# Experts fed by 512-column units of gate, then of up, and their activations turned one unit later

## The chip, the cores and the metric

The kernel runs on one core of a Trainium2 chip. The metric is the device time of one execution in microseconds (us), lower is better. Engines: TensorE (PE, with its weight loads PEld), VectorE (DVE), ScalarE (ACT), GpSimd (POOL) and SyncE (SP, here the queue that issues nearly all loads).

## What is computed

Two transformer blocks over 256 tokens of width 1024, in float32. The second layer of the first block ends in a mixture of experts, and that is the part that changes:

```python
def swiglu(h, wg, wu, wd):
    return (jax.nn.silu(h @ wg) * (h @ wu)) @ wd

def moe_swiglu(h, router, wg, wu, wd):
    logits = (h @ router).astype(jnp.float32)
    top_vals, top_idx = lax.top_k(logits, TOP_K)          # TOP_K = 2
    gates = jax.nn.softmax(top_vals, axis=-1)
    ...
    for e in range(N_EXPERTS):                            # N_EXPERTS = 8
        out = out + gate_e[..., e:e + 1] * swiglu(h, wg[e], wu[e], wd[e])
    return out
```

Each expert has wg and wu of 1024 x 3584 and wd of 3584 x 1024: 44 MB of weights for each, 352 MB in all, of the 629 MB that the kernel reads.

## The kernel before

Every weight is split into a high and a low part in a reduced-precision format (ACT copies the high part, DVE subtracts to get the low part), and each product is three matmuls: high by high, high by low, low by high. So a megabyte that comes in costs one ACT and one DVE instruction before TensorE can use it.

**Units.** `feed` runs an expert as NB1 = 14 units. Unit n loads 256 columns of gate and 256 of up into one slot of `ringA` (two slots of 2 MB, each in two halves `h` over the 1024 rows), and 256 rows of down into a slot of `ringB` (two slots of 1 MB). The halves are split into `As` (one buffer for each half, high and low), the down rows into `Bs` (one buffer). A half is filled by two loads of 512 KB with runs of 1 KB, one from gate and one from up. If at most 128 tokens chose any expert (the `If` at L1083, taken here), the tokens of expert e are gathered into `xgs` and all products have one tile of 128 rows (T = 1). The other branch (`Else`, T = 2) isn't run with this input.

**TensorE in a unit** (`body` in `feed`): 12 matmuls on half 0 (`gu(i, u, 0)`, L806), the turn of the previous unit's activations (`turn`, 2 transposes, L819), 12 matmuls on half 1, 12 matmuls with `Bs` for the previous unit (`down`, L834). After some units come the scatter of the previous expert's result (L884, units 2 and 3) and the gather for the next (L871, unit 12).

**ScalarE in a unit:** copy of the turned activations (L1518, `hds`), high part of the next unit's half 0 (L1497), silu of this unit's gate (L1535), high part of the next unit's half 1, high part of this unit's down rows (L1545). **VectorE:** low part of `hds` (L2092), low part of half 0 (L2077), silu times up (L2108), low part of half 1, low part of the down rows (L2114, signals `B_low`).

**Order of the loads.** SP is one in-order queue. For unit pairs i it issues A(i, 0), B(i-1, 1), A(i, 1), B(i, 0) (`load_experts`). A load of half h waits until that half of the slot's last content has been split (`A_split`); a load of down rows waits for `B_low` of the block before it. After the last expert `load_ffn` follows for the next stage, `ff0c`, whose first two units' halves are also split by the experts' last units (ACT L1497 and DVE L2077 of "the next unit").

**Ends.** The first unit has no down products. In the last unit of the last expert TensorE turns its own unit's activations, runs four idle products (`idle_products(4)`, L690) and then the last down products. `keep_y` (ACT L1574) then copies the sum out, `scatter` and `add` (L884, L2150) put it into the residual stream.

Of the kernel before, what the change touches and what calls it, by code (L numbers as in the profile page):

```python
# [24 lines left out]
ALU = mybir.AluOpType  # L25
# [3 lines left out]
P = 128  # L29
SEQ = 256  # L30
D = 1024
KC = D // P
# [100 lines left out]
def build(nc, t, out, AT1, N1, AT2, N2):  # L133
    ctx = ExitStack()
    with ctx:
# [90 lines left out]

        xgT = ar(0, KC, P)
# [4 lines left out]
        chosen = ar(2816, TILES, NE)  # L232

# [124 lines left out]
        def ffn(name, nb, times=1):  # L358
            nonlocal b, s, f, q, xc
            ph[name] = dict(a=a, b=b, s=s, f=f, nb=nb, td=through, q=q, xc=xc)  # L360
            SPLIT.update((a + n, q + n) for n in range(nb * times))
            take(nb * times, 2, TILES)
# [19 lines left out]
        ffn("moe", NB1, NE)  # L382
# [65 lines left out]
        def blocks(eng, nb, body, head=1):  # L448

            m = (nb - 1) // 2  # L450
            for i in range(head):
                body(i, 0, False)
                body(i, 1, False)
            with eng.Fori(head, m) as i:
                body(i, 0, False)
                body(i, 1, False)
            for n in range(2 * m, nb):
                body(m, n % 2, n == nb - 1)

# [37 lines left out]
        def _(sp):  # L497
# [71 lines left out]
            def load_experts(p, wg, wu, wd):  # L569
# [3 lines left out]
                def A(e, i, u):  # L573
                    n, a0 = i * 2 + u, p["a"] + u
                    g, up = wg(e), wu(e)
# [68 lines left out]
            load_ffn(ph["ff0c"], *g0)  # L644
# [38 lines left out]
        def _(pe):  # L683
# [177 lines left out]

            def gather(e):
# [24 lines left out]
            def expert(e):  # L887
# [13 lines left out]
                feed(moe, lambda l, tt, k: xgs[:, l, k, :], 1, e, 2 * e + 1, xg_split, after, head=2, leads=first, drains=final)  # L901
# [192 lines left out]
            with pe.Else():  # L1094
                with pe.Fori(0, NE - 1) as e:
                    feed(moe, split_stream, 2, e, 1, xr_split)
                feed(moe, split_stream, 2, NE - 1, 1, xr_split)
# [305 lines left out]
        def _(act):  # L1403
# [161 lines left out]

            def rows_part(e, h):
# [9 lines left out]
            def expert(e):  # L1576
# [3 lines left out]
                def before(n):  # L1580
                    if n == 1 and not first:
                        keep_y(e - 1)
# [3 lines left out]
                feed(ph["moe"], 1, e, True, 2, first, final, before, None if final else lambda h: rows_part(e + 1, h))  # L1586
# [160 lines left out]
            with act.Else():  # L1747
                act.wait_ge(pn_lo, PN["ffn1"]["lo"] + 2)
                x_parts(hT, None, xr_high)
                with act.Fori(0, NE - 1) as e:  # L1750
                    feed(ph["moe"], 2, e, True)
                feed(ph["moe"], 2, NE - 1, True)
# [226 lines left out]
        def _(dve):  # L1979
# [142 lines left out]

            def acc(tt):
# [34 lines left out]
            def expert(e):  # L2158
# [15 lines left out]
                feed(ph["moe"], 1, e, True, 2, first, final, after, None if final else lambda h: rows_part(e + 1, h))  # L2174
# [264 lines left out]
            with dve.Else():  # L2439
                def all_tokens(e):  # L2440
                    feed(p, 2, e, True)
# [323 lines left out]
```

## Time and profile before

| | us |
|---|---|
| median of three runs | 2700.34 |
| lowest, highest | 2695.68, 3695.21 |
| the profiled execution | 2695.8 |
| its span in the profile | 2694.0 |
| PE busy, DVE busy, ACT busy | 2573.2, 1820.4, 1456.5 |
| mean granted TensorE clock | 0.975 of full speed |

The experts lie between 613 us (first matmul of the first expert) and 1634 us (end of the last down products). In a row of the timeline the columns are start, duration, engine, line, operation, output and inputs and count; what stands in brackets is the idle time of the engine before it and what ended that.

### The profile page before, as it was taken

How to read it: one execution, taken by the hardware profiler on the slowest of the kernel's cores; microseconds unless marked ns; L12 is line 12 of the kernel's file. 1: busy time of each engine (PE TensorE's matmuls, PEld its weight loads, DVE VectorE, ACT ScalarE, POOL GpSimd, SP SyncE). 2: the span in 40 equal slices, each digit the busy share in tenths (PEclk: the TensorE clock that was granted, in tenths of full speed). 3: DMA queues.
4: the chain of work that ended last, by engine and by line, in shares of the span. 5: the costliest groups of instructions: out<-in, count | busy, mean ns of one | idle time of the engine just before them, and what ended most of it. 6: DMA issues, size and time to landing. Idle time of an engine off the chain costs nothing.

```text
span 2694.0 us, 34481 instructions
## 1 busy us (share of the span) xinstructions
PE 2573.2 (96%) x11981; PEld 2031.8 (75%) x11981; DVE 1820.4 (68%) x1810; ACT 1456.5 (54%) x1677; POOL 52.2 (2%) x40
## 2 busy tenths in 40 slices
PE   7899999878999999999999998999999999998998
PEld 6678887656878787878888886888884687776786
DVE  6454446548888988888888885545444475776544
ACT  4544434535677777777777675445333243466443
POOL 0000000015000000000000000000000000000000
PEclk9999999879999999999999999999999999998999
DMA  6865542659999999999999996555543344435551
GB/s 217 290 219 187 187 156 87 241 179 308 367 336 353 348 351 349 352 349 351 349 346 355 339 343 203 181 185 184 183 156 108 102 142 127 130 107 179 184 186 60
DMA packets 446014, 631.66 MB, mean 234 GB/s; under 512 B 17672, under 2 KB 345896, under 8 KB 445736
## 3 DMA queue, kind: packets, MB, share of 16 engines
q1 hardware_dynamic: 445064, 627.36, 69.5%
q0 software_dynamic: 864, 3.15, 0.3%
q8 instruction: 55, 0.90, 0.1%
q14 instruction: 31, 0.25, 0.0%
HBM read 629.40 MB, written 1.05 MB: 234 GB/s over the span
## 4 chain that ended last, share of the span: by engine, by line
PE 87%; DVE 6%; ACT 4%; issue 2%; DMA 1%; SPq 0%; DVEq 0%; ACTq 0%
PE ps L806 39%; PE ps L834 20%; PE ps L1188 6%; PE ps L740 5%; PE ps L1215 2%; PE ps L1120 2%; PE ps L819 2%; PE ps L930 1%; PE ps L871 1%; DVE As L2077 1%; PE ps L1179 1%; DVE ringL L2047 1%; PE ps L884 1%; ACT Bs L1545 1%; ACT As L1497 1%
## 5 line engine op out<-in xcount | busy, mean ns | idle before, releaser
L2077 DVE TENSOR_TENSOR As<-ringA,As 128x2048 fp32r<-128x2048 f32 x318 | 735.2, 2312 | 212.4 <-ACT As L1497 203.5
L806 PE MATMUL ps<-As,xgs 128*128 128x512 f32 x2688 | 666.1, 397 | 6.7 <-DVE As L2077 4.1
L1497 ACT ACTIVATE As<-ringA 128x2048 fp32r<-128x2048 f32 x318 | 608.0, 1912 | 22.7 <-DMA ringA<-in_dense_w_up 9.9
L834 PE MATMUL ps<-Bs,hds 128*128 128x512 f32 x2472 | 590.0, 391 | 12.3 <-DVE hds L2092 12.3
L806 PEld LDWEIGHTS ps<-As,xgs 128*128 128x128 f32 x2688 | 494.7, 188 | 117.5 <-issue 14.3
L834 PEld LDWEIGHTS ps<-Bs,hds 128*128 128x128 f32 x2472 | 464.1, 188 | 116.5 <-issue 9.2
L2114 DVE TENSOR_TENSOR Bs<-ringB,Bs 128x2048 fp32r<-128x2048 f32 x159 | 368.8, 2320 | 157.4 <-ACT Bs L1545 156.8
L1545 ACT ACTIVATE Bs<-ringB 128x2048 fp32r<-128x2048 f32 x159 | 304.9, 1918 | 215.6 <-PE ps L834 215.4
L806 PE MATMUL ps<-As,xs 128*128 128x512 f32 x1632 | 392.3, 397 | 10.8 <-DVE xs L2015 6.8
L806 PEld LDWEIGHTS ps<-As,xs 128*128 128x128 f32 x1632 | 306.3, 190 | 78.3 <-issue 7.6
L1518 ACT ACTIVATE hds<-ps 128x256 fp32r<-128x256 f32 x206 | 73.9, 383 | 317.5 <-PE ps L819 282.8
L1535 ACT ACTIVATE sg<-ps 128x256 f32<-128x256 f32 x206 | 79.1, 384 | 192.9 <-PE ps L806 168.7
L2092 DVE TENSOR_TENSOR hds<-ps,hds 128x256 fp32r<-128x256 f32 x206 | 82.2, 418 | 90.1 <-ACT hds L1518 89.5
L2047 DVE TENSOR_TENSOR ringL<-ringA,ringH 128x2048 fp32r<-128x2048 f32 x42 | 96.1, 2290 | 57.3 <-ACT ringH L1477 57.1
L740 PE MATMUL ps<-As,xs 128*128 128x512 f32 (+1 forms) x384 | 118.7, 393 | 9.4 <-DVE ringL L2047 5.6
L2108 DVE TENSOR_TENSOR hh<-sg,ps 128x256 f32<-128x256 f32 x206 | 85.3, 415 | 55.8 <-ACT sg L1535 55.7
L1477 ACT ACTIVATE ringH<-ringA 128x2048 fp32r<-128x2048 f32 x42 | 80.2, 1911 | 79.2 <-PE ps L1188 57.7
L806 PE MATMUL ps<-As,hcTR 128*128 128x512 f32 x352 | 111.6, 398 | 0.0
L740 PEld LDWEIGHTS ps<-As,xs 128*128 128x128 f32 x384 | 73.8, 198 | 25.1 <-DVE ringL L2047 6.0
L1188 PE MATMUL ps<-ringL,hcTR 128*128 128x512 f32 x224 | 87.6, 391 | 0.0
L740 PE MATMUL ps<-ringL,xs 128*128 128x512 f32 (+1 forms) x224 | 87.2, 389 | 0.0
L1188 PE MATMUL ps<-ringH,hcTR 128*128 128x512 f32 x208 | 83.3, 401 | 0.8 <-DVE ringL L2047 0.8
(349 smaller groups left out, 2632.4 us busy)
## 6 DMA issues: line engine op xcount, KB each, us to landing
ringA<-in_moe_w_gate SPq DMA_DIRECT2D x224, 512.0 KB, 4.5
ringA<-in_moe_w_up SPq DMA_DIRECT2D x224, 512.0 KB, 5.6
ringB<-in_moe_w_down SPq DMA_DIRECT2D x112, 1024.0 KB, 6.2
ringA<-in_w_ff_in SPq DMA_DIRECT2D x132, 512.0 KB, 4.7
ringA<-in_w_in SPq DMA_DIRECT2D x56, 1024.0 KB, 5.3
ringA<-in_w_ada SPq DMA_DIRECT2D x36, 1024.0 KB, 6.2
ringB<-in_w_ff_out SPq DMA_DIRECT2D x33, 1024.0 KB, 5.0
ringA<-in_dense_w_gate SPq DMA_DIRECT2D x28, 512.0 KB, 3.6
```

The source lines that it names most:

```text
L740: m = mm(ps[:, 4 + 2 * (n % 2) + tt, 0:cols], xs[:, l, k, tt * P:(tt + 1) * P], w, start=k == 0 and m_ == 0, stop=k == KC - 1 and m_ == 2)
L806: m = mm(ps[:, bank, :], lhs(l, tt, k), As[:, h, r, k % 4, :], start=k == 0 and n == 0, stop=k == KC - 1 and n == 2)
L834: m = mm(ps[:, 4 + 2 * tt + half, :], hds[:, buf, l, q, :], Bs[:, q, r, half * 512:(half + 1) * 512], start=first and q == 0 and n == 0, s ...
L1188: m = mm(dst, lhs[l][:, k, tt * P:(tt + 1) * P], w[q], start=k == 0 and m_ == 0, stop=k == KC - 1 and m_ == 2)
L1477: A(high(p["name"], n, h)[:, :, 0:cols], ringA[:, a0 % 2, 4 * h:4 * h + 4, 0:cols], ACT.Copy).then_inc(A_high, 1)
L1497: A(As[:, h, 0, :, :], ringA[:, (p["a"] + u) % 2, 4 * h:4 * h + 4, :], ACT.Copy).then_inc(A_high, 1)
L1545: A(Bs[:, :, 0, :], ringB[:, b0 % 2, :, :], ACT.Copy).then_inc(B_high, 1)
L2047: V.tensor_tensor(ringL[:, a0 % 2, 4 * h:4 * h + 4, 0:cols], ringA[:, a0 % 2, 4 * h:4 * h + 4, 0:cols], f32(high(p["name"], n, h)[:, :, 0: ...
L2077: V.tensor_tensor(As[:, h, 1, :, :], ringA[:, (p["a"] + u) % 2, 4 * h:4 * h + 4, :], f32(As[:, h, 0, :, :]), ALU.subtract).then_inc(A_spli ...
L2092: V.tensor_tensor(flat(hds[:, buf, 1, :, :]), ps[:, 2 + tt, 0:FB], f32(flat(hds[:, buf, 0, :, :])), ALU.subtract).then_inc(hdT_ready, 2 // T)
L2108: V.tensor_tensor(hh[:, buf, :], sg[:, buf, :], ps[:, buf, FB:BW], ALU.mult).then_inc(h_ready, 2 // T)
L2114: V.tensor_tensor(Bs[:, :, 1, :], ringB[:, (p["b"] + u) % 2, :, :], f32(Bs[:, :, 0, :]), ALU.subtract).then_inc(B_low, 1)
```

## The change

The diff has four parts.

1. A unit is now 512 columns of gate (u = 0) or 512 columns of up (u = 1). A half is one load of 1 MB with runs of 2 KB. Bytes, splits and matmuls stay the same in number.
2. Silu and the product with up are done once for a pair of units, on 128x512 instead of twice on 128x256. The activations of a pair are turned in the two units of the next pair, and the down products follow them there: TensorE's down products of a block of rows come one unit later, and so do the splits of the down rows on ACT and DVE. `keep_y` moves from unit 1 to unit 2.
3. In the last pair of the last expert the first down block of that pair is split into other buffers (`down_home`: high into `hTR`, low in place in `ringB`'s slot), the products with the block before it are cut in two around the turns, and the idle products are gone. The next stage's first load of down rows waits until that slot is free.
4. The branch for all tokens (not run here) is written anew.

```diff
-                        sp.dma_start(ringA[:, a0 % 2, sl, 0:FB], w2d(g)[:, sl, bass.ds(n * FB, FB)]).then_inc(A_full[a0 % 2][h], 16)
-                        sp.dma_start(ringA[:, a0 % 2, sl, FB:BW], w2d(up)[:, sl, bass.ds(n * FB, FB)]).then_inc(A_full[a0 % 2][h], 16)
+                        sp.dma_start(ringA[:, a0 % 2, sl, :], w2d((wg, wu)[u](e))[:, sl, bass.ds(i * BW, BW)]).then_inc(A_full[a0 % 2][h], 16)
...
-            load_ffn(ph["ff0c"], *g0)
+            load_ffn(ph["ff0c"], *g0, ring=(down_done, ph["ff0c"]["s"] - 2))
...
+                def body(i, u, last):
+                    lead = first and isinstance(i, int) and i == 0
+                    gate_or_up(e, i, u, 0, 1, lambda l, tt, k: xgs[:, l, k, :], 2 * e + 1, xg_split)
+                    if not lead:
+                        turn_part(e, i - 1, u, 1)
+                    gate_or_up(e, i, u, 1, 1, lambda l, tt, k: xgs[:, l, k, :], 2 * e + 1, xg_split)
+                    if last and final:
+                        down_part(e, i - 1, u, 1, qs=(0,))
+                        turn_part(e, i, 0, 1)
+                        pe.wait_ge(selgT_ready, e + 1)
+                        turn_part(e, i, 1, 1, 3, False)
+                        down_part(e, i - 1, u, 1, qs=(1,))
+                        down_part(e, i, 0, 1, down_home(moe, moe["b"]))
+                        down_part(e, i, 1, 1)
+                    elif not lead:
+                        down_part(e, i - 1, u, 1)
+                    if isinstance(i, int):
+                        after(2 * i + u)
+                blocks(pe, NB1, body, 2)
...
+                def body(i, u, last):
...
+                    if not lead:
+                        part_high(e, i - 1, u, 1)
+                    unit_high(e, *nxt, 0)
+                    if last and not final:
+                        rows_part(e + 1, 0)
+                    if u == 0:
+                        gate_silu(e, i, 1)
+                    unit_high(e, *nxt, 1)
...
+                    if last and final:
+                        down_high(e, i, 0, down_home(ph["moe"], ph["moe"]["b"])[0], 0)
+                        part_high(e, i, 0, 1)
+                        part_high(e, i, 1, 1, 3)
+                        down_high(e, i, 1, None, 2)
+                    elif u:
+                        down_high(e, i, 0)
+                    elif not lead:
+                        down_high(e, i - 1, 1)
...
+                def body(i, u, last):
...
+                    if not lead:
+                        part_low(e, i - 1, u, 1)
+                    unit_low(e, *nxt, 0)
+                    if last and not final:
+                        rows_part(e + 1, 0)
+                    if u:
+                        gate_times_up(e, i, 1)
+                    unit_low(e, *nxt, 1)
...
+                    if last and final:
+                        down_low(e, i, 0, down_home(ph["moe"], ph["moe"]["b"]))
+                        part_low(e, i, 0, 1)
+                        part_low(e, i, 1, 1, 3)
+                        down_low(e, i, 1)
+                    elif u:
+                        down_low(e, i, 0)
+                    elif not lead:
+                        down_low(e, i - 1, 1)
```

`gate_or_up`, `turn_part` and `down_part` are TensorE's old `gu`, `turn` and `down` with the new counts; `unit_high`, `part_high`, `gate_silu`, `down_high` (ACT) and `unit_low`, `part_low`, `gate_times_up`, `down_low` (DVE) are the steps of the old `body` taken apart. The order of SP's loads and the condition of each stay as they were.

## Rows read from the trace of the kernel before

**Rows 1.** The page, busy time of each engine over the span.
```profile
PE 2573.2 (96%) x11981; PEld 2031.8 (75%) x11981; DVE 1820.4 (68%) x1810; ACT 1456.5 (54%) x1677; POOL 52.2 (2%) x40
```
**Rows 2.** Waits, 640:1600: engine, line, what for, us in total, times, longest.
```profile
PE ps L834 <- DVE hds L2092: 5.4, 8, 2.6
```
**Rows 3.** Groups by line and form, 640:1600: busy us, mean ns, idle before.
```profile
L2077 DVE TENSOR_TENSOR As<-ringA,As 128x2048 fp32r<-128x2048 f32 x214 | 495.0, 2313 | 75.9 <-ACT As L1497 67.0
L1497 ACT ACTIVATE As<-ringA 128x2048 fp32r<-128x2048 f32 x213 | 407.3, 1912 | 0.0
...
L1569 ACT ACTIVATE xgs<-arena 128x512 fp32r<-128x512 f32 x14 | 8.6, 617 | 0.0
...
L2145 DVE TENSOR_TENSOR arena<-ps,vcol 128x512 f32<-128x512 f32 x14 | 9.0, 681 | 0.0
```
**Rows 4.** Windows: stretch, its us, busy of each engine, PEclk, DMA share, GB/s.
```profile
31.00:35.00 4.00, 4.00 (x19) 3.25 (x18) 3.27 (x18) 0.10 (x1) 0.00 (x0) 1.00 1.03 380
700.00:1600.00 900.00, 898.48 (x4098) 729.47 (x4097) 796.34 (x595) 646.67 (x529) 0.00 (x0) 1.00 1.03 350
...
1656.00:1660.00 4.00, 4.00 (x19) 3.30 (x18) 2.61 (x5) 3.95 (x6) 0.00 (x0) 1.00 0.00 0
1012.00:1016.00 4.00, 4.00 (x19) 3.34 (x18) 3.85 (x3) 3.02 (x3) 0.00 (x0) 1.00 1.06 383
```
**Rows 5.** Timeline of one steady unit, 1006.48 to 1014.91, and what follows.
```profile
1006.48 2.88 PE L806 MATMUL ps<-As,xgs 128*128 128x512 f32 x12
...
1009.34 3.02 PE L806 MATMUL ps<-As,xgs 128*128 128x512 f32 x12
...
1009.95 1.91 ACT L1497 ACTIVATE As<-ringA 128x2048 fp32r<-128x2048 f32 x1
...
1012.19 2.88 PE L834 MATMUL ps<-Bs,hds 128*128 128x512 f32 x12
...
1012.72 1.91 ACT L1497 ACTIVATE As<-ringA 128x2048 fp32r<-128x2048 f32 x1
...
1014.91 2.88 PE L806 MATMUL ps<-As,xgs 128*128 128x512 f32 x12
...
1017.12 2.29 DVE L2114 TENSOR_TENSOR Bs<-ringB,Bs 128x2048 fp32r<-128x2048 f32 x1 [0.17 <-ACT Bs L1545]
...
1019.67 0.37 SPq L590 DMA_DIRECT2D ringB<-in_moe_w_down  x1
```
**Rows 6.** DMA issues: tiles, queue, count, KB each, median us to landing.
```profile
ringA<-in_w_in SPq DMA_DIRECT2D x56, 1024.0 KB, 5.3
```
**Rows 7.** Timeline, the first expert's units 0, 1 and 2.
```profile
613.19 5.80 PE L806 MATMUL ps<-As,xgs 128*128 128x512 f32 x24 [2.56 <-DVE xgs L2156]
...
620.66 2.97 PE L806 MATMUL ps<-As,xgs 128*128 128x512 f32 x12 [1.67 <-DVE As L2077]
...
632.55 3.01 PE L806 MATMUL ps<-As,xgs 128*128 128x512 f32 x12 [1.11 <-DVE As L2077]
```
**Rows 8.** Timeline, the last expert's units 12 and 13 and its end.
```profile
1603.56 8.67 SPq L590 DMA_DIRECT2D ringB<-in_moe_w_down  x2
...
1607.32 2.88 PE L806 MATMUL ps<-As,xgs 128*128 128x512 f32 x12
...
1615.90 3.00 PE L806 MATMUL ps<-As,xgs 128*128 128x512 f32 x12
...
1619.76 1.92 ACT L1497 ACTIVATE As<-ringA 128x2048 fp32r<-128x2048 f32 x1 [0.17 <-DMA ringA<-in_w_ff_in]
...
1623.92 0.41 DVE L2108 TENSOR_TENSOR hh<-sg,ps 128x256 f32<-128x256 f32 x1
...
1624.11 1.91 ACT L1497 ACTIVATE As<-ringA 128x2048 fp32r<-128x2048 f32 x1 [1.46 <-DMA ringA<-in_w_ff_in]
...
1630.93 3.00 PE L834 MATMUL ps<-Bs,hds 128*128 128x512 f32 x12 [2.67 <-DVE hds L2092]
```
**Rows 9.** Windows around a pause of PE after the experts, columns as in rows 4.
```profile
1644.00:1648.00 4.00, 0.00 (x0) 0.00 (x0) 0.96 (x1) 2.05 (x3) 0.00 (x0) 0.78 0.03 8
1648.00:1652.00 4.00, 3.59 (x9) 2.85 (x10) 1.57 (x3) 3.72 (x6) 0.00 (x0) 0.50 0.00 0
```

More of the change, by code:

```diff
@@ new lines, in down_part @@
+            def down_part(e, i, u, T, weights=None, qs=range(2)):
+                first = isinstance(i, int) and i == 0 and u == 0
+                for tt in range(T):
+                    if first and tt == 0:
+                        pe.wait_ge(acc_free, e + moe["f"])
+                    pe.wait_ge(hdT_ready, ffn_count(moe, T, e, i, u, tt))
+                    if tt == 0:
+                        pe.wait_ge(B_low, e * NB1 + i * 2 + (moe["b"] + u + 1))
+                    for q in qs:
+                        for n, (l, r) in enumerate(((0, 0), (0, 1), (1, 0))):
+                            for half in range(2):
+                                m = mm(ps[:, 4 + 2 * tt + half, :], hds[:, u if T == 1 else tt, l, q, :], (Bs[:, q, r, :] if weights is None else weights[r][:, q, :])[:, half * 512:(half + 1) * 512],
+                                       start=first and q == 0 and n == 0, stop=q == 1 and n == 2, skip_group_check=True)
+                    if 1 in qs:
+                        m.then_inc(down_done, 2 // T)
@@ L862, in gather, with all_tokens @@
+            def all_tokens(e):
+                def body(i, u, last):
+                    for h in range(2):
+                        gate_or_up(e, i, u, h, 2, split_stream, 1, xr_split)
+                    if u:
+                        for part in range(2):
+                            turn_part(e, i, part, 2)
+                            down_part(e, i, part, 2)
+                blocks(pe, NB1, body)
             def gather(e):
@@ new lines, in part_high @@
+            def part_high(e, i, u, T, bank=2):
+                p = ph["moe"]
+                for tt in range(T):
+                    act.wait_ge(tp_done, ffn_count(p, T, e, i, u, tt))
+                    v = ffn_count(p, T, e, i, u, tt, 3 - T)
+                    if started(v):
+                        act.wait_ge(down_done, v)
+                    A(hds[:, u if T == 1 else tt, 0, :, :].rearrange("p a b -> p (a b)"), ps[:, bank if T == 1 else tt, 0:FB], ACT.Copy).then_inc(hd_high, 2 // T)
@@ new lines, in gate_silu, with down_high @@
+            def gate_silu(e, i, T):
+                p = ph["moe"]
+                for tt in range(T):
+                    act.wait_ge(tile_done, thru(p, T, e, i, 0, tt))
+                    v = ffn_count(p, 2, e, i - 1, 1, 1)
+                    if started(v):
+                        act.wait_ge(h_ready, v)
+                    A(sg[:, :, :].rearrange("p u n -> p (u n)") if T == 1 else sgW[:, tt, :], ps[:, tt, :], ACT.Silu).then_inc(silu_done, 4 // T)
+            def down_high(e, i, u, dst=None, back=1):
+                p = ph["moe"]
+                b0 = p["b"] + u
+                act.wait_ge(B_full[b0 % 2], e * (8 * NB1) + i * 16 + 16 * (b0 // 2 + 1))
+                v = ffn_count(p, 2, e, i, u, 1, back)
+                if back and started(v):
+                    act.wait_ge(down_done, v)
+                A(Bs[:, :, 0, :] if dst is None else dst, ringB[:, b0 % 2, :, :], ACT.Copy).then_inc(B_high, 1)
@@ new lines, in all_tokens @@
+            def all_tokens(e):
+                def body(i, u, last):
+                    nxt = (i + 1, 0) if u else (i, 1)
+                    for h in range(2):
+                        unit_high(e, *nxt, h)
+                    if u == 0:
+                        gate_silu(e, i, 2)
+                        down_high(e, i, 0)
+                    else:
+                        part_high(e, i, 0, 2)
+                        down_high(e, i, 1)
+                        part_high(e, i, 1, 2)
+                blocks(act, NB1, body)
```

129 lines of the change are left out of this document (114 added, 15 removed).

## Prediction, made before the changed kernel was run

> **What bounds the kernel now.** I read the page first. TensorE is busy for 96% of the span, the next engine, VectorE, for 68% [rows 1]. But an average over stages proves little, so the second view is the windows. Over 900 us of expert work PE is busy for 898.48 us, at full clock, while the DMA engines stand at a share of 1.03 and move 350 GB/s [rows 4]. Two resources look full there, and the reader has to see which of them is late. The waits answer it. In 640 to 1600 us PE waited for a vector result 8 times, 5.4 us in all [rows 2], and ScalarE's high parts, which are the first users of a load, had an idle time of 0.0 us before 213 of them [rows 3]. So no load was late; the DMA engines are busy but ahead, and TensorE sets the pace. Does the traffic slow the matmuls? With a DMA share of 0.00 PE began 19 matmuls in 4 us, with 1.06 it also began 19 [rows 4]. It doesn't.
>
> The timeline gives the unit. Half 0 with the turn takes 1009.34 - 1006.48 = 2.86 us, half 1 2.85 us, down 1014.91 - 1012.19 = 2.72 us, together 8.43 us [rows 5], 16.86 us for a pair. All of this is products that the change keeps.
>
> **Part 1, the loads.** Two loads of 512 KB become one of 1 MB, with packets of 2 KB. In 31 to 35 us only such packets flowed, at the same share of 1.03, and gave 380 GB/s against the experts' 350 [rows 4]. So 3.15 MB for a unit, which take about 8.4 us now, would take about 8.0. Since no load is late, this is worth 0 by itself; its cover is the queue's lead. The Trainium skill (DMA: Bandwidth & Descriptors, Why small descriptors are slow) names a fixed overhead for each packet, and the two rates agree with its direction. By that rule alone, if the loads had set the pace, the experts would be 8% quicker at best; the 0.0 us speaks against that.
>
> **Part 2, silu and product on 512 columns.** Removed for a pair: two silus and two products on 128x256, the product 0.41 us each [rows 8]. Added: one on 128x512, for which the nearest rows are 0.62 us on ACT and 0.68 us on DVE [rows 3]. DVE gains 0.82 - 0.68 = 0.14 us per pair, off the path. But the one product is longer and stands ahead of the low part of half 1 in odd units, and the one silu ahead of the high part in even units, so half 1 is ready about 0.25 us later. Its margin now: the high part starts 1012.72 - 1006.48 = 6.24 us into the unit, which plus 1.91 and 2.29 us is 10.44, against 8.43 + 2.86 = 11.29 us when PE wants it. 0.85 us become about 0.6. In the steady loop this costs 0. At the seven changes of expert, where the next rows' parts go through both engines too, I charge 0.25 us each, **+1.8 us** (bounds 0 and 5).
>
> **Part 3, the first expert starts with two units that have no down products.** PE now comes to unit 1 at 620.66 and to unit 2 at 632.55, 11.9 us later [rows 7], with unit 1's down products in between and DVE slowed beside POOL. Without the down work unit 2 should start one unit-without-down later, as unit 1 did: 620.66 - 613.19 = 7.5 us, and a little more for the slower DVE, 9.0 us. That is about 3 us earlier. The down products aren't saved, they are done at the far end, where I count them. **-3 us** (bounds -6 and 0).
>
> **Part 4, the split of the down rows comes one unit later: in the loop.** This is where the change can hurt. A load of down rows waits for `B_low` of the block before, and on SP two halves of the next unit are queued behind it. Now `B_low` falls at 1017.12 + 2.29 = 1019.41, that is 4.5 us into a unit, and SP issues 0.26 us later [rows 5]; the halves behind it become free only later, so nothing is held up. In the changed kernel that `B_low` belongs to the block one unit back, which makes the queue wait one unit longer for the same block. SP then issues the down rows and both halves at one go, 3.15 MB, 4.8 us into each unit. High parts of the halves start 3.47 us (1009.95 - 1006.48) and 6.24 us into the unit after it, so the loads have 8.43 + 3.47 - 4.8 = 7.1 and 9.9 us of lead.
>
> When do they land? An unhurried 1 MB load takes 5.3 us [rows 6]; the two behind it follow at 380 GB/s, 2.76 us each. So the first half lands 8.1 us and the second 10.8 us after the issue, each some 1 us late; 0.6 to 0.8 us of that are margin. Now the loop that closes once a pair: `B_low` of block (i-1, 1), issue 0.26, second half landed 10.8, high part 1.91, low part 2.29, split of the down rows 2.29, that is `B_low` of (i, 1). The sum is 17.5 us against PE's 16.86. If the first load lands in 5.0 and the others flow at the best rate seen, the sum is 17.1; if they share nothing and land 1 us sooner it is 16.5, and PE still sets the pace. The excess is thus between 0 and 0.65 us per pair. Of the seven pairs of an expert about two are forgiven (the 0.6 us margin, and gather and scatter give PE more to do at the change of expert), so for 8 experts and 5 pairs the bounds are 0 and 26 us. I take the middle, **+12 us**: the loop is the thing nearest to both limits and no row shows a burst of three such loads in flight.
>
> **Part 5, the end of the last expert.** Here the late `B_low` isn't covered. Now SP issues the last down rows at 1603.56 + 8.67 - 0.37 = 1611.86, and the loads of `ff0c` stand behind them. Their first half is there at 1619.76 and their second at 1624.11 [rows 8]. One unit later is 1615.90 - 1607.32 = 8.58 us, so they land at 1628.34 and 1632.69. ACT and DVE split them ahead of the experts' own last steps:
>
> - first half: high 1628.3 to 1630.3, low to 1632.6, then the product of silu and up, 0.68, to 1633.3. PE, done with unit 13 at 1615.90 + 5.71 = 1621.6 and with half of the waiting down products at 1623.0, is idle until 1633.3, about 10 us.
> - second half: high 1632.7 to 1634.6, the down rows' high part 1.91 to 1636.5; DVE low part to 1636.9, the down rows' low part to 1639.2, two parts of `hds` 0.82 to 1640.0 (the first at 1639.6).
> - PE runs the first of the last two down blocks from 1639.6 to 1642.4. The last block's low part is done at 1640.0 + 2.29 = 1642.3, its products at 1645.1.
>
> Now the last down products end at 1630.93 + 2.72 = 1633.65 [rows 8], the idle products already inside. The end moves by **+11.5 us** (bounds 5, if the loads land 6 us sooner without other traffic, and 13). After it `keep_y`, scatter and add follow as before. What is late next is `ff0c`: its data has long been there, so it inherits the whole delay.
>
> A pause of PE has a second price. After the experts PE is idle for some 7 us; in 1644 to 1648 the granted clock falls from 1.00 to 0.78 and in 1648 to 1652 it is 0.50 [rows 9], the 1.2 GHz level. A 10 us pause in the new place should do the same, and a down block then takes 2.72 us more. One of two blocks is on the path: **+1.5 us** (0 to 5.4). The Trainium skill (TensorE: Matmul & The Clock Gate, HAM oscillation) says the same of matmul bursts separated by waits; the rows agree.
>
> **Sum.** 1.8 - 3 + 12 + 11.5 + 1.5 = +23.8 us. The profiled execution took 2695.8, so 2719.6. The undisturbed runs of before are 2695.7 and 2700.3 (the median shown, 2700.34, is the upper of them), so I say **2720 us**, +0.8%.
>
> **Rivals.**
> 1. *The loop isn't late* (chance 0.35). The burst lands in time because the bigger packets leave the DMA engines idle before each burst. Then only start and end count: 2695.8 + 1.8 - 3 + 13 = 2707.6. For it: 0.0 us of waiting on loads today. Against it: the loop's sum lies at or above 16.86 with every row that I can use.
> 2. *The loop sets the pace outright* (0.17). If the three loads take 12 us together, as three loads in a row behind each other do before `ff0c` (1624.11 - 1611.86 = 12.25 [rows 8], with 1 KB packets), the loop is 18.9 us, 2.1 us over, and with 5 to 6 pairs of 8 experts it costs 84 to 100 us beside the 12 us of the other terms: 2790 to 2810. Halfway it gives 2750. It makes the kernel slower by 2% (54 us, of which 42 here, 1.05 us for each of 40 pairs) from a landing at 11.2 us on.
> 3. *Faster* (0.08). The next stage's loads don't hold the end up, since the transfers land 8 us sooner once nothing else is in flight; then the end also loses the wait of 2.67 us ahead of the last down products [rows 8], and with the earlier start the kernel takes 2695.8 - 3 - 2.7 = 2690. The point from which it decides: the first half must be there by 1621, which needs an issue by 1613, one unit before its turn in the queue. That is why I give it little. The Trainium skill (DMA: Bandwidth & Descriptors, Bandwidth) recommends loads of 1 MB and more, which would put the change on this side; its gain is in transfers that hide already.
>
> My forecast (loop late by up to 26 us) has 0.40. The range that leaves out 2 in 10 reaches from the first rival to the lower half of the second: **2700 to 2750**. By 2% (54 us, about what a measurement of this kernel can tell from no change): faster 0.02, same 0.90, slower 0.08.
>
> **What would show it.** Part 5: an idle time of PE ahead of the turn of the last pair, ended by DVE, near 10 us, and ACT waiting for `in_w_ff_in`; the end of the last down products near 1645 less the start's gain. Part 4: ACT's high parts get idle time ended by a load of `in_moe_w_gate` or `in_moe_w_up`, now 0.0; pairs of 17.0 to 17.5 us instead of 16.86. Part 3: the first expert's unit 2 starts near 630. Part 1: GB/s over the experts unchanged but DMA share near 0.95. If the queue's loads are early, part 4 is wrong; if PE's pause at the end is under 3 us, part 5 is.

## The result, and the profile after

| | before | changed |
|---|---|---|
| median (lowest to highest), us | 2698.34 (2690.16 to 3695.21) | 2725.36 (2716.95 to 2730.57) |
| runs | 7 | 7 |
| ratio of the undisturbed runs | | 1.0098, 95% interval 1.0082 to 1.0115 |
| span of the profiled execution, us | 2694.0 | 2723.6 |

The changed kernel is 1.0% slower, 27 us by the medians and 29.6 us between the two profiled executions. One of the seven runs of the kernel before, at 3695.21 us, was disturbed and isn't in the ratio. The page of the changed kernel (busy time, share of the span and instructions of each engine) answers [rows 1]:

```profile
PE 2588.1 (95%) x11973; PEld 2033.2 (75%) x11973; DVE 1802.6 (66%) x1754; ACT 1457.4 (54%) x1621; POOL 51.2 (2%) x40
```

DVE has 18 us less work, and the kernel is slower all the same. To see where the 29.6 us came from, the span is cut at matmuls that both kernels have:

| stretch | longer by, us | predicted |
|---|---|---|
| up to the first expert matmul | -0.65 | 0 |
| from there to unit 2 of the first expert | -4.2 | -3 |
| from there to unit 13 of the last expert | +19.3 | +13.8 |
| unit 13 to the first matmul behind the last down products (17.9, now 29.3) | +11.5 | +13 |
| from there to the first matmul of `ff0c` | -2.3 | 0 |
| `ff0c` and all behind it, whose code is the same | +6.0 | 0 |

**The loop.** The same stretch of 900 us as in [rows 4], in the windows of the changed kernel (stretch, its us, busy of PE, PEld, DVE, ACT, POOL, clock, DMA share, GB/s):

```profile
700.00:1600.00 900.00, 891.26 (x4021) 712.35 (x4020) 767.62 (x536) 634.53 (x470) 0.00 (x0) 1.00 0.94 343
```

PE is idle for 8.7 us in place of 1.5, and 77 fewer matmuls fit (4021 against 4098), about 17 us of work at 0.22 us each. PE's idle time shows only 7 us of that. The rest stands in the waits of the weight loads (PEld) below, beside which PE is recorded as busy. From one `keep_y` to the next an expert takes 127.8 to 129.5 us, most often 128.2, where it took 126.15. The DMA engines do less, 0.94 against 1.03: the 2 KB packets do carry the same bytes with less engine time. Yet loads are now late. The waits of 640 to 1640 us (engine, line, what for; us in total, times, longest), against [rows 2, 3], where ACT's high parts waited 0.0 us:

```profile
ACT As L1666 <- DMA ringA<-in_moe_w_gate: 48.3, 64, 2.1
...
PEld ps L889 <- DVE As L2249: 22.6, 43, 1.8
...
ACT As L1666 <- DMA ringA<-in_moe_w_up: 15.2, 29, 2.2
...
PE ps L889 <- DVE As L2249: 7.2, 15, 1.4
```

A full share of the DMA engines with no wait has become a smaller share with 93 waits. That points away from how much is moved, and to when it is asked for; the experiments have to show it. The page's DMA issues (tiles, queue, count, KB each, median us to landing) point the same way: 8.5 and 9.0 us from issue to landing, and the timeline shows one burst.

```profile
ringA<-in_moe_w_gate SPq DMA_DIRECT2D x112, 1024.0 KB, 8.5
ringA<-in_moe_w_up SPq DMA_DIRECT2D x112, 1024.0 KB, 9.0
ringB<-in_moe_w_down SPq DMA_DIRECT2D x112, 1024.0 KB, 5.0
```
```profile
1005.25 2.29 DVE L2324 TENSOR_TENSOR Bs<-ringB,Bs 128x2048 fp32r<-128x2048 f32 x1
...
1007.56 0.37 SPq L601 DMA_DIRECT2D ringB<-in_moe_w_down  x1
...
1008.39 1.00 SPq L594 DMA_DIRECT2D ringA<-in_moe_w_gate  x2
...
1015.33 1.92 ACT L1666 ACTIVATE As<-ringA 128x2048 fp32r<-128x2048 f32 x1 [0.70 <-DMA ringA<-in_moe_w_gate]
...
1018.01 1.92 ACT L1666 ACTIVATE As<-ringA 128x2048 fp32r<-128x2048 f32 x1 [0.76 <-DMA ringA<-in_moe_w_gate]
...
1020.09 2.28 DVE L2249 TENSOR_TENSOR As<-ringA,As 128x2048 fp32r<-128x2048 f32 x1
...
1022.29 2.29 DVE L2324 TENSOR_TENSOR Bs<-ringB,Bs 128x2048 fp32r<-128x2048 f32 x1
...
1024.81 0.37 SPq L601 DMA_DIRECT2D ringB<-in_moe_w_down  x1
```

Follow it from the top. DVE ends the low part of a block of down rows at 1007.54; SP issues the next rows at 1007.56 and both halves of the next unit within 1.8 us. ACT waits for the halves, which are there at 1015.33 and 1018.01, 7.8 and 10.4 us after the first issue. Then high part, low part, low part of the down rows, and SP's next issue for the same slot at 1024.81, 17.25 us after the last. PE's work in a steady pair is 16.86 us [rows 5]. The fourth to sixth pair of an expert are steady, with neither gather nor scatter: from the second expert on they took 16.87 us each before and take 16.9 to 18.2 us now, 17.34 us in the mean.

**The end of the last expert**, against [rows 8]:

```profile
1626.75 8.37 SPq L601 DMA_DIRECT2D ringB<-in_moe_w_down  x2
...
1630.34 3.00 PE L889 MATMUL ps<-As,xgs 128*128 128x512 f32 x12
...
1642.74 1.91 ACT L1666 ACTIVATE As<-ringA 128x2048 fp32r<-128x2048 f32 x1 [8.71 <-DMA ringA<-in_w_ff_in]
...
1645.76 1.91 ACT L1666 ACTIVATE As<-ringA 128x2048 fp32r<-128x2048 f32 x1 [1.11 <-DMA ringA<-in_w_ff_in]
1646.89 0.68 DVE L2317 TENSOR_TENSOR hh<-sg,ps 128x512 f32<-128x512 f32 x1
...
1647.62 1.12 PE L904 MATMUL ps<-c,hh 128*128 128x128 f32 x4 [9.93 <-DVE hh L2317]
...
1648.39 2.91 PE L919 MATMUL ps<-Bs,hds 128*128 128x512 f32 x6
...
1656.91 2.93 PE L919 MATMUL ps<-Bs,hds 128*128 128x512 f32 x12
```

Before, the first half of the next stage's second unit was there 3.86 us after unit 13 began [rows 8]; now 12.40 us after. ACT waits for it for 8.71 us. The experts' own last steps stand behind it in program order, so PE has nothing to do for 9.93 us. Six down matmuls then take 2.91 us, double their time at full clock; the windows show the clock that was granted:

```profile
1640.00:1644.00 4.00, 0.00 (x0) 0.00 (x0) 0.00 (x0) 1.26 (x1) 0.00 (x0) 0.76 1.10 358
1644.00:1648.00 4.00, 0.38 (x2) 0.38 (x3) 3.19 (x3) 2.89 (x3) 0.00 (x0) 0.50 1.10 348
```

### The profile page after: what moved, and what is told of

Read it like the earlier page. It is cut to its first block, busy times and chain, and to the rows that moved or that the text cites. A ratio compares the mean times of both kernels' runs of the same rounds, so it can differ in the third digit from the quotient of the medians.

```text
span 2723.6 us, 33592 instructions
## 1 busy us (share of the span) xinstructions
PE 2588.1 (95%) x11973; PEld 2033.2 (75%) x11973; DVE 1802.6 (66%) x1754; ACT 1457.4 (54%) x1621; POOL 51.2 (2%) x40
## 3 DMA queue, kind: packets, MB, share of 16 engines
q0 software_dynamic: 864, 3.15, 0.3%
## 4 chain that ended last, share of the span: by engine, by line
PE 66%; DVE 12%; DMA 8%; ACT 7%; issue 5%; SPq 1%; DVEq 0%; ACTq 0%
PE ps L817 18%; PE ps L845 9%; PE ps L889 8%; DMA ringA<-in_moe_w_gate 6%; PE ps L1280 6%; PE ps L751 5%; DVE As L2249 4%; PE ps L919 4%; ACT As L1666 3%; DVE Bs L2324 3%; PE ps L1307 2%; PE ps L1212 2%; DMA ringA<-in_moe_w_up 2%; PE ps L1022 1%; PE ps L944 1%
## 5 line engine op out<-in xcount | busy, mean ns | idle before, releaser
L889 PE MATMUL ps<-As,xgs 128*128 128x512 f32 x2688 | 672.3, 400 | 17.5 <-DVE As L2249 12.7
L817 PEld LDWEIGHTS ps<-As,xs 128*128 128x128 f32 x1632 | 306.0, 189 | 76.2 <-DVE hh L2280 5.9
L2324 DVE TENSOR_TENSOR Bs<-ringB,Bs 128x2048 fp32r<-128x2048 f32 x111 | 253.8, 2287 | 4.2 <-ACT Bs L1696 3.2
L2286 DVE TENSOR_TENSOR Bs<-ringB,Bs 128x2048 fp32r<-128x2048 f32 x47 | 107.7, 2292 | 139.5 <-ACT Bs L1637 139.5
L1627 ACT ACTIVATE sg<-ps 128x256 f32<-128x256 f32 x94 | 36.1, 384 | 130.9 <-PE ps L817 129.9
```

Of the source, the lines that this page charges most:

```text
L817: m = mm(ps[:, bank, :], lhs(l, tt, k), As[:, h, r, k % 4, :], start=k == 0 and n == 0, stop=k == KC - 1 and n == 2)
L889: m = mm(ps[:, bank, :], lhs(l, tt, k), As[:, h, r, k % 4, :], start=k == 0 and n == 0, stop=k == KC - 1 and n == 2)
L2286: V.tensor_tensor(Bs[:, :, 1, :], ringB[:, (p["b"] + u) % 2, :, :], f32(Bs[:, :, 0, :]), ALU.subtract).then_inc(B_low, 1)
L2324: V.tensor_tensor(lo, ringB[:, (p["b"] + u) % 2, :, :], f32(hi), ALU.subtract).then_inc(B_low, 1)
```

## Experiments

The theory: SP issues in order, and a load of down rows that waits for a `B_low` which now comes a unit later holds back what is queued behind it, in each unit and once more at the end. Rivals: the bigger packets themselves, and the wider silu and product.

### The order of the loads, in the loop and at the end

`e1` turns the order in the loop so that a wait that falls a unit later stands a unit later in the queue. `e2` does it for the last rows only, and `e3` both.

```diff
 def rest(e):
-    A(e, 0, 1)
-    B(e, 0, 0)
     with sp.Fori(1, nb // 2) as i:
         A(e, i, 0)
-        B(e, i - 1, 1)
+        B(e, i - 1, 0)
         A(e, i, 1)
-        B(e, i, 0)
+        B(e, i - 1, 1)
...
 A(0, 0, 0)
+A(0, 0, 1)
 rest(0)
 with sp.Fori(1, NE) as e:
     A(e, 0, 0)
+    B(e - 1, nb // 2 - 1, 0)
+    A(e, 0, 1)
     B(e - 1, nb // 2 - 1, 1)
     rest(e)
+B(NE - 1, nb // 2 - 1, 0)
 B(NE - 1, nb // 2 - 1, 1)
```

For `e2` the last `B(NE - 1, nb // 2 - 1, 1)` goes behind `A(1, 0, 1)` of `load_ffn`; for `e3` that and, between the next stage's two units, `B(NE - 1, nb // 2 - 1, 0)`.

> The changed kernel, in which only SP's order within the experts is another: each load of down rows is issued after the next unit's gate or up instead of ahead of it (A(i,0), B(i-1,0), A(i,1), B(i-1,1)), so that no load of gate or up stands behind a wait for down rows that is fulfilled later. The next stage's loads still stand behind the experts' last down rows. Theory (the queue's order makes the loop late): ScalarE's high parts wait no longer for loads of gate or up, pairs take 16.87 us again instead of 17.4, an expert 126.1 us instead of 128.2, so 15 us less than the changed kernel over eight experts (about 2710), while the pause of PE of 10 us after the last up products stays. Rival (the engines' margin, eaten up by silu and product on 512 columns, makes the loop late): pairs stay at 17.4 us and the time at 2725. Rival (transfers of 1 MB are too slow, whenever they are issued): high parts still wait for loads.

> The changed kernel, in which only the end of the queue is another: the next stage's first two units are issued ahead of the experts' last down rows. Theory: PE's pause of 10 us before the turn of the last pair goes, the last down products end about 10 us earlier (at 19 us after the start of unit 13 instead of 29), the clock doesn't fall there, pairs stay at 17.4 us: 10 us less than the changed kernel, about 2715. Rival (the end is long because of its own new work: two splits of down rows and two pairs of turned parts after the last product): 2 us less at most.

> Both orders of the two runs beside it in one kernel. Theory: the gains add up, 15 + 10 = 25 us less than the changed kernel, 2700, level with the kernel before (2698) within 5 us; it may be up to 5 us better than before, since the first expert's unit 2 starts 4 us earlier. Rival (something else in the change costs time, for instance more work at the change of expert): 2710 or more.

The last column is the stretch from the first expert matmul to the first matmul of `ff0c` in the profiled execution. The code ahead of it and behind it is the same in all kernels and differs by some us from one execution to the next, so this column shows the effects most cleanly.

| | median, us | to before, 95% | steady pair, mean (range), us | PE's pause before the last turn | experts to `ff0c`, us |
|---|---|---|---|---|---|
| before | 2697.33 | | 16.87 | | 1035.2 |
| changed | 2725.36 | 1.0098 (1.0082 to 1.0115) | 17.34 (16.9 to 18.2) | 9.93 | 1059.5 |
| e1 | 2703.10 | 1.0012 (0.9999 to 1.0024) | 16.87 | 9.90 | 1042.4 |
| e2 | 2716.94 | 1.0071 (1.0054 to 1.0088) | 17.42 (16.9 to 18.0) | 2.00 | 1055.0 |
| e3 | 2694.75 | 0.9991 (0.9982 to 1.0001) | 16.87 | 1.12 | 1033.1 |

The issues of `e1` on its page (up is alike, with 5.2 us), and its 900 us in the windows:

```profile
ringA<-in_moe_w_gate SPq DMA_DIRECT2D x112, 1024.0 KB, 5.1
```
```profile
700.00:1600.00 900.00, 897.31 (x4087) 727.45 (x4087) 782.79 (x545) 641.14 (x478) 0.00 (x0) 1.00 0.96 349
```

Nothing but the order is changed, and the landing falls from 8.5 to 5.1 us. The timeline of its queue shows what is different: a load goes out every 2.4 to 3.2 us, where the changed kernel issues three within 1.8 us.

```profile
1002.87 0.37 SPq L594 DMA_DIRECT2D ringA<-in_moe_w_up  x1
1005.29 0.37 SPq L601 DMA_DIRECT2D ringB<-in_moe_w_down  x1
1008.50 3.12 SPq L594 DMA_DIRECT2D ringA<-in_moe_w_gate  x2
1013.69 0.37 SPq L601 DMA_DIRECT2D ringB<-in_moe_w_down  x1
```

In `e1` the wait for a load of gate or up is gone from the list of waits, and an expert takes 126.5 us, where the changed kernel took 128.2 and the kernel before 126.15. But the pause at the end is whole, in `e1`'s timeline:

```profile
1628.61 1.12 PE L906 MATMUL ps<-c,hh 128*128 128x128 f32 x4 [9.90 <-DVE hh L2319]
```

and in `e2`'s it is the other way round:

```profile
1635.63 0.66 PE L908 MATMUL ps<-c,hh 128*128 128x128 f32 x4 [2.00 <-DVE hh L2321]
```

So there are two separate costs with one cause. By the medians `e1` is 22 us below the changed kernel (15 were expected) and `e2` 8 us (10); in the last column it is 17.1 and 4.4 us, and 26.4 for `e3`; the rest lies in code that is the same. The two gains thus don't just add up: in `e2`, whose loop is still late, the end took 23.3 us from the start of unit 13, in `e3` 20.2. Two of `e2`'s expectations missed, 19 us for that end and a clock that doesn't fall. `e3` is at the kernel before or a little under it. Both orders together take the whole loss back while packets and widths stay changed, so neither of these made it.

### The size of the packets

`e4` is the changed kernel with each half as two loads of 512 KB with runs of 1 KB; `e6` is the same edit on `e3`.

```diff
-sp.dma_start(ringA[:, a0 % 2, sl, :], w2d((wg, wu)[u](e))[:, sl, bass.ds(i * BW, BW)]).then_inc(A_full[a0 % 2][h], 16)
+for c in range(2):
+    sp.dma_start(ringA[:, a0 % 2, sl, c * FB:(c + 1) * FB], w2d((wg, wu)[u](e))[:, sl, bass.ds(i * BW + c * FB, FB)]).then_inc(A_full[a0 % 2][h], 16)
```

> The changed kernel with each load of 1 MB cut into two of 512 KB with packets of 1 KB, as before, in the changed order of work. Theory: three megabytes in a row take 2.6 + 2 x 3.0 us instead of 2.6 + 2 x 2.7, so the second half lands about 0.6 us later and a pair takes 17.9 to 18.0 us instead of 17.4; over 5 to 7 pairs of eight experts 22 to 34 us more than the changed kernel, 2750. Rival (one load of 1 MB lands later for its first user than two of half the size): faster than the changed kernel. Rival (loads are not what the loop waits for): 2725.

> The kernel with both orders, each load of 1 MB cut into two of 512 KB with packets of 1 KB. Theory (packet size is worth nothing where loads are a unit ahead): high parts don't wait for loads, pairs 16.87 us, an expert 126.5 us, time 2695 within 3 us, although the same cut cost the changed kernel 10 us and 1.7 us per expert. Rival (smaller packets load the DMA engines until they are late): pairs over 17 us, 2705 or more.

`e4` took 2735.62 us, ratio 1.0134 (1.0117 to 1.0151): 10 us more than the changed kernel. The second half lands 0.6 us later in steady units, as expected (11.1 us after the issue of the down rows, against 10.5), and a steady pair takes 17.76 us, nearly the 17.9 to 18.0 expected. The whole missed: an expert takes 1.8 us more (130.0 against 128.2) and not 3 to 4, because only a part of its seven pairs are late. `e4`'s waits:

```profile
ACT As L1667 <- DMA ringA<-in_moe_w_gate: 72.4, 75, 2.6
```

`e6` took 2695.91 us, ratio 0.9994 (0.9984 to 1.0004), against 2694.75 for `e3`: nothing, with a DMA share of 1.02 in place of 0.96 at the same 349 GB/s. The bigger packets are worth something only where loads are late, and there they soften what the order costs.

### More to move: a dose

128 KB more behind each load of down rows, 14.7 MB in all, on the changed kernel (`e7`) and on `e3` (`e8`). The extra bytes go to a part of `arena` that nothing reads; all of the computation is done.

```diff
+x0 = e * (16 * nb) + i * 32 + 16 * u
+if started(x0):
+    sp.wait_ge(extra, x0)
+sp.dma_start(arena[:, 18192:18448], t["w_hy_out_2"][0:P, 0:256]).then_inc(extra, 16)
```

> The changed kernel with one more transfer of 128 KB (1 KB packets, into unused memory, 0.37 us of the 16 engines) right behind each load of down rows and so ahead of the two halves. Theory (issue, landing of the third load, high part, low part, down rows' split close a loop once a pair): the halves land 0.35 to 0.4 us later and a pair takes that much longer, 17.75 us instead of 17.38; an expert 2 us more than 128.2, in all 16 us more than the changed kernel, 2741. Rival (the engines' margin, not the loads, sets the pair): no change, 2725.

> The same additional transfers in the kernel with both orders. Theory: the loads have a lead of more than their landing, so pairs stay at 16.87 us and the time at 2695, although as many bytes are moved as in the run beside it. Rival (it is the DMA engines' total work that costs time): as much more as in the run beside it, about 16 us.

`e7` took 2779.91 us, ratio 1.0300 (1.0276 to 1.0325), 55 us more than the changed kernel, at a DMA share of 0.94. `e8` took 2693.44 us, ratio 0.9986 (0.9975 to 0.9996), at a higher share:

```profile
700.00:1600.00 900.00, 897.28 (x4087) 727.30 (x4086) 783.31 (x543) 641.37 (x478) 0.00 (x0) 1.00 0.99 363
```

This separates the two readings of "DMA bound". If bytes per second were the limit, both would have grown, `e8` the more. Only the kernel whose loads come in a burst did. But I had expected 16 us, not 55. The dose delays the burst by more than its bytes, since it is one more issue between the down rows and the halves:

```profile
1106.67 0.37 SPq L602 DMA_DIRECT2D ringB<-in_moe_w_down  x1
1107.20 0.35 SPq L606 DMA_DIRECT2D arena<-in_w_hy_out  x1
1108.41 1.03 SPq L595 DMA_DIRECT2D ringA<-in_moe_w_gate  x2
```

Here the halves are issued 1.74 us after the rows; over the steady units it is 1.36 us in the mean, in the changed kernel 0.84. And the flight is longer too: the second half lands 12.2 us after the issue of the rows, where it took 10.5. That is 1.7 us later, of which 0.5 is the issue; I had priced 0.37. The loop passes it on whole: a steady pair takes 19.1 us against 17.34, and an expert 134.3 to 137.2. Why 128 KB lengthen the flight by 1.2 us isn't known. The matmuls that wait:

```profile
PE ps L895 <- DVE As L2255: 51.9, 50, 2.8
```

### Silu and product in two pieces

`e9` is `e3` with one silu and one product of 512 columns cut into two of 256.

```diff
-A(sg[:, :, :].rearrange("p u n -> p (u n)") if T == 1 else sgW[:, tt, :], ps[:, tt, :], ACT.Silu).then_inc(silu_done, 4 // T)
+dst = sg[:, :, :].rearrange("p u n -> p (u n)") if T == 1 else sgW[:, tt, :]
+for c in range(2):
+    m = A(dst[:, c * FB:(c + 1) * FB], ps[:, tt, c * FB:(c + 1) * FB], ACT.Silu)
+m.then_inc(silu_done, 4 // T)
```

> The kernel with both orders, with silu and product of a pair as two instructions on 128x256 each instead of one on 128x512, at the same places. This makes what stands ahead of the splits longer once more, by 0.14 us on VectorE and 0.16 us on ScalarE. Theory (part 2 of the change costs nothing in steady pairs and its length at each change of expert): pairs stay at 16.87 us; an expert, which takes 126.5 us against 126.15 before, takes 0.1 to 0.2 us more, 126.65. Rival (part 2 has no part in the 0.35 us): 126.5 unchanged.

2692.62 us in one run. Experts take 126.54 to 126.62 us, `e3`'s 126.5, those of the kernel before 126.15. Two pieces cost 0.05 to 0.1 us per expert more than one, a little under the 0.1 to 0.2 expected. But this doesn't clear the width. Before, one product of 256 columns stood in each unit; now a unit with u = 1 has all 512, in one instruction of 0.68 us or in two of 0.41. The timelines show what that costs. What `e3` has left over the kernel before lies in the first pair of each expert, 17.42 us against 17.07, and there half 1 waits for the new expert's rows (`xgs`). The kernel before, whose unit began at 1250.12:

```profile
1249.92 0.41 DVE L2108 TENSOR_TENSOR hh<-sg,ps 128x256 f32<-128x256 f32 x1
...
1252.45 0.68 DVE L2156 TENSOR_TENSOR xgs<-arena,xgs 128x512 fp32r<-128x512 f32 x1
...
1253.19 3.02 PE L806 MATMUL ps<-As,xgs 128*128 128x512 f32 x12
```

and `e3`, whose unit began at 1241.15:

```profile
1241.02 0.68 DVE L2322 TENSOR_TENSOR hh<-sg,ps 128x512 f32<-128x512 f32 x1
...
1243.82 0.69 DVE L2364 TENSOR_TENSOR xgs<-arena,xgs 128x512 fp32r<-128x512 f32 x1
...
1244.56 3.06 PE L894 MATMUL ps<-As,xgs 128*128 128x512 f32 x12 [0.16 <-DVE xgs L2364]
```

Half 1 begins 3.41 us after half 0, before 3.07. Of the 0.34 us, 0.27 are the longer product, which DVE runs ahead of the rows. In `e9` half 1 begins after 3.46 us.

### The next stage's splits behind the experts' own

In `e3` ACT and DVE still split the next stage's second unit ahead of the experts' last down rows. `e5` puts these splits last.

```diff
-                    unit_high(e, *nxt, 0)
+                    if not (last and final):
+                        unit_high(e, *nxt, 0)
...
                         down_high(e, i, 1, None, 2)
+                        for h in range(2):
+                            unit_high(e, *nxt, h)
```

and the same for the half 1 and for `unit_low`.

> The kernel with both orders, in which the last pair of the last expert splits the next stage's first two halves after the experts' own last down rows instead of ahead of them. Theory (in-order work for the next stage still holds up the end): in the profile with both orders the first of the last two down blocks waits 2.7 us for hds and starts at 1621.24, the last at 1625.48, with unit 13 at 1608.03; now the last block starts as soon as its rows have landed and are split, some 3.8 us earlier, 13.7 us after the start of unit 13 instead of 17.5, and the kernel takes about 2691, 0.2 to 0.3% less than before. Rival (the end is bound by the landing of the last down rows): no gain.

2695.12 us, ratio 0.9996 (0.9985 to 1.0008). Missed: nothing gained over `e3`, the rival's outcome. Its timeline tells what took the gain:

```profile
1617.57 0.37 SPq L605 DMA_DIRECT2D ringB<-in_moe_w_down  x1
...
1625.97 1.91 ACT L1701 ACTIVATE Bs<-ringB 128x2048 fp32r<-128x2048 f32 x1 [3.12 <-DMA ringB<-in_moe_w_down]
...
1630.35 5.46 PE L924 MATMUL ps<-Bs,hds 128*128 128x512 f32 x12 [4.67 <-DVE Bs L2333]
```

The last down rows landed 8.4 us after their issue, behind the next stage's second unit (issued from 1612.3 to 1616.2). PE waited 4.67 us, and the last block took 5.46 us at a granted clock of 0.50 (1630 to 1634). No wait in the queue held the rows back this time: they went out 0.03 us after their slot was free (DVE's low part ended at 1617.54). What is left is the 2 MB ahead of them in flight, the order of issue again, in a place where I hadn't looked for it. So `e11` issues both sets of last down rows ahead of that unit:

```diff
-return (lambda: B(NE - 1, nb // 2 - 1, 0)), (lambda: B(NE - 1, nb // 2 - 1, 1))
+return (lambda: (B(NE - 1, nb // 2 - 1, 0), B(NE - 1, nb // 2 - 1, 1))), (lambda: None)
```

> The kernel of e5 with the last four issues of the experts' end in another order: the next stage's first unit, both sets of the last down rows, then the next stage's second unit (in e5 both units stood ahead of the rows). All of the computation is done. Theory (in e5 the end was set by the last down rows, which landed 8.4 us after their issue behind the second unit, 4.67 us of waiting and then a block at half clock, 5.46 us in place of about 2.9): the rows land near 5 us after their issue, the wait of TensorE for DVE Bs falls from 4.67 us to about 1, the last block takes near 3 us, and the time falls by about 6 us to 2689, 0.3% below the kernel before. Rival (something else ends the stage, such as the turn of the next stage's second unit or the branch behind it): 2695, as e3 and e5.

```profile
1610.55 8.88 SPq L605 DMA_DIRECT2D ringB<-in_moe_w_down  x2
...
1624.23 1.91 ACT L1701 ACTIVATE Bs<-ringB 128x2048 fp32r<-128x2048 f32 x1
...
1628.61 2.97 PE L924 MATMUL ps<-Bs,hds 128*128 128x512 f32 x12 [1.43 <-DVE Bs L2333]
```

2691.64 us beside 2697.47 of the kernel before, ratio 0.9977 (0.9965 to 0.9989): 0.2% below the kernel before, the lowest of the versions that were timed several times. The last rows go out at 1619.06, as long after the start of unit 13 as in `e5`, and land in less than 5.2 us; the granted clock stays at 1.00. From the start of unit 13 to the first matmul behind the last down products it is 16.8 us (1614.66 to 1631.42) against 22.4 in `e5` (1613.17 to 1635.60), 20.2 in `e3` and 17.9 in the kernel before. So 5.7 of the 6 us expected are there; the medians show 3.5, the ratios 5. From the first expert matmul to that of `ff0c` this kernel takes 1030.8 us, 4.4 less than the kernel before; 2.3 of these come from the branch of the next section and not from the way the experts are fed.

### The branch behind the experts

The next stage's first matmul comes 2.3 us sooner behind the last add than before, which no step of mine had. In the kernel before:

```profile
1641.70 1.22 DVE L2150 TENSOR_TENSOR x<-x,ps 128x1024 f32<-128x1024 f32 x1 [2.15 <-PE ps L884]
...
1645.95 2.00 ACT L1507 ACTIVATE xs<-hcT 128x1024 fp32r<-128x1024 f32 x2 [10.96 <-DVEq L2453]
```

3.03 us pass between the add's end and ACT, which waits for a signal that DVE's queue gives behind the `If`; in the changed kernel 0.73. `e10` is the kernel before with the branch for all tokens left out, which this input doesn't take (with another input it would compute nothing there).

```diff
-            with dve.Else():
-                def all_tokens(e):
...
```

> The kernel before, without the branch for more than 128 tokens of an expert, which this input doesn't take. It leaves nothing out of what runs here. Question: after the experts the kernel before takes 3.03 us from the last add's end to the first copy of the next stage's rows, the changed kernels 0.73 us. Theory (VectorE's jump over the branch that isn't taken costs time, and the change made that branch's code shorter): 0.7 us here too, 2.3 us less in the span. Rival (the gap comes from something in the taken branch): 3.0 us as before.

```profile
1635.47 1.22 DVE L2140 TENSOR_TENSOR x<-x,ps 128x1024 f32<-128x1024 f32 x1 [2.15 <-PE ps L884]
...
1637.04 2.00 ACT L1503 ACTIVATE xs<-hcT 128x1024 fp32r<-128x1024 f32 x2 [8.27 <-DVEq L2429]
```

The gap is 0.35 us. So getting past that branch cost 2.7 us before and 0.4 in the rewritten one. That it passes on DVE's queue is read from the profile, since `e10` leaves the branch out on all three engines. The run took 2687.53 us beside 2697.56; 5.5 of the 8.4 us between the two profiles lie ahead of the experts, where the two codes are the same, and aren't the branch's.

## Why the prediction was right, and where it wasn't

The time, 2725.4 us, lies in the range and 5 us from the 2720 forecast. The steps one by one:

- **Part 1, the loads, 0.** Right: DMA share 0.94 (0.95 was named), and `e6` against `e3` gives 0 with the two sizes. Not quite complete: in the late loop the size counts, 10 us in `e4`. The comparison of 380 with 350 GB/s was a misreading: 350 is what the experts ask for, 3.15 MB in a unit of 9.0 us in the mean, and in 1012 to 1016 the same mix of packets moved 383 [rows 4]. What the packets save shows in the share at one rate, 0.96 against 1.02.
- **Part 2: +1.8.** 2.0: with the order of the loop mended, `e1` and `e3` take 985.4 and 985.3 us from unit 2 of the first expert to unit 13 of the last, where the kernel before took 983.35. The steady pair costs nothing, 16.87 us in both, as said. The cost lies at the change of expert, 0.35 us where I charged 0.25, and the timelines beside `e9` show it: the longer product stands ahead of the next rows.
- **Part 3: -3.** -4.2. Unit 2 starts at 627.68, named was "near 630". For a unit without down products I took the row's 7.5 us and added 1.5 for a slower DVE; it took 7.7.
- **Part 4: +12, bounds 0 and 26.** The mechanism is shown by `e1`, and its times too: landings 7.8 and 10.4 us after the first issue (8.1 and 10.8), loop 17.25 us (17.1 to 17.5). From unit 2 to unit 13 the kernel lost 19.3 us, of which 2.0 are part 2, so the term is 17.3 and not 12. What was mis-sized: I took half of the upper excess, 0.3 us for a pair and 12 us for 40 pairs; a steady pair took 0.48 more (17.34 against 16.87). Nor was it five pairs of seven: nearly all of an expert's loss lies in its three steady pairs and the first one, and the pairs with gather or scatter forgive most of it (20.06 against 19.92, 17.83 unchanged). The first expert lost 1.9 us of the 19.3. One case of the sum was off as well: with the first load in 5.0 us and the others at 2.76 it comes to 17.3 us, not 17.1.
- **Part 5: +11.5, and +1.5 for the clock.** Together 11.5 measured. First half 12.40 us after unit 13's start (12.44), pause 9.93 us (10), granted clock 0.50 in 1644 to 1648. The second half came sooner than I had it, 15.42 us and not 16.79, which gave back what the clock took. The row of before gave 12.25 us from the issue of the down rows to that half, now it was 11.01; why isn't known. The half clock cost about what I had charged: the block ahead of the last one took 4.33 us (1652.58 to 1656.91), at full clock it takes 2.72, so 1.6 us. A much shorter pause can bring it: in `e2` PE paused for 2.00 us, and the granted clock was 0.56 in 1636 to 1640 and 0.50 in 1640 to 1644.
- **Not in the sum.** -2.3 us for the branch, shown by `e10`. And +6.0 us in code that is the same in both. The windows from the first matmul of `ff0c` to the end, of before, of the changed kernel and of `e5`:

```profile
1648.41:2694.00 1045.59, 1004.66 (x4602) 785.27 (x4602) 588.30 (x662) 457.29 (x584) 0.00 (x0) 0.98 0.46 148
```
```profile
1672.01:2723.60 1051.59, 1009.92 (x4602) 790.01 (x4602) 588.62 (x662) 457.29 (x584) 0.00 (x0) 0.98 0.46 147
```
```profile
1648.01:2693.70 1045.69, 1004.89 (x4602) 786.28 (x4602) 588.63 (x662) 457.30 (x584) 0.00 (x0) 0.98 0.46 148
```

The same 4602 matmuls keep PE busy for 5.3 us longer in the changed kernel, while DVE and ACT do the same. `e5`, which has the changed code, is back at 1045.7. So this isn't the change. Over the thirteen traces this code takes 1045.6 to 1051.6 us: in three of them 1045.6 to 1046.1, with the lower clock granted for 42 to 43 us of it, in the other ten 1048.5 to 1051.6, with 45 to 54 us. The runs of one kernel differ in the same way: of the changed kernel's seven the quickest, 2716.95 us, has a mean granted clock of 0.977 and the slowest, 2730.57, of 0.971. What decides that isn't known. The total owes part of its nearness to 2720 to luck: to `ff0c` I had +23.8 and 23.6 were measured, made of terms that are off by +5.3 (part 4), +0.2 (part 2), -1.5 (part 5), -1.2 (part 3), -0.65 (the start) and -2.3 (the branch).

**The rivals.** "The loop isn't late" fell with 93 waits of ACT on loads. "The loop sets the pace outright" needed a landing at 11.2 us; it was 10.4. `e7` shows how near that was: 128 KB more in each burst make the landing 12.2 us and the kernel 3.0% slower than before. "Faster" needed the first half of the next stage's second unit by 1621 in the old numbering; it came at 1628.3 there, 8.5 us later than before against unit 13. The recommendation of loads of 1 MB and more in the Trainium skill (DMA: Bandwidth & Descriptors, Bandwidth) gave nothing here while the loads led: 2694.75 us with 1 MB, 2695.91 with 512 KB.

## What to carry to other kernels

When a change moves the instruction that frees a buffer, read the in-order queue of the loads next: find the load that waits for it, and list what stands behind it. A load that can't go yet belongs behind those that can, at the end of a stage too. And a load whose first user comes early shouldn't go out behind big loads that are needed later (`e5`, `e11`). A full share of the DMA engines is no sign that transfers set the pace, nor a lower one that they don't: the idle time ahead of a load's first user tells.

## What the hardware showed that I hadn't expected

- A load's time to landing depends more on what was issued with it than on its size: 1 MB with 2 KB runs took 5.1 us when a load went out every 2.4 to 3.2 us (`e1`), 8.5 to 9.0 as a median in bursts of three, at a lower average rate (343 against 349 GB/s).
- PE's wait of 4.67 us ahead of one block cost 2.5 us more in the block itself, 5.46 us at a granted clock of 0.50 against 2.97 us at 1.00 behind a wait of 1.43 us (`e5`, `e11`).
- Passing a branch that wasn't taken cost 2.7 us before (`e10`), 0.4 in the changed kernel.
- Identical code took 1045.6 to 1051.6 us. The three quickest traces had the lower clock for 42 to 43 us of it, the others for 45 to 54.
